# Re-queueing the mixers of a two-block kernel: sigmoids, gates, convolution taps and one-column sums

## The reference

```python
p_pool, p_bval, p_bgate, p_cgate, p_cx = jnp.split(_rmsnorm(h, mix_norm_g) @ w_in, splits, axis=-1)
# A: windowed means of p_pool, one small product, a scale
# B: u = p_bval * sigmoid(p_bgate); causal depthwise convolution of 31 taps over 256 channels;
#    layernorm over the channels; silu; one 256x256 product
# C: xc = 4-tap convolution of p_cx (512 channels); r, i = sigmoid(xc @ w_a + b_a), sigmoid(xc @ w_x + b_x)
#    log_a = -8 * r * softplus(-lam); a = exp(log_a); h = scan(a, sqrt(1 - a*a) * (i * xc)); gelu(p_cgate) * h
h = h + concat([A, B, C]) @ w_out
h = h + square(relu(_rmsnorm(h, mlp_norm_g) @ w_up)) @ w_down
```

## Time and profile before

| | before |
|---|---|
| median of 3 runs | 1047.05 us (1046.64 to 1047.58) |
| the profiled execution, its own time | 1047.22 us |
| its span, first to last instruction | 1045.3 us |
| busy PE, DVE, ACT, POOL | 98%, 49%, 40%, 55% |
| mean granted TensorE clock | 0.991 |

### The profile page before, as it was taken

One profiled execution on the slowest core, in us unless ns is written; L12 is line 12 of the kernel. 1 busy time (PEld: TensorE's weight loads), 2 busy tenths in 40 slices (PEclk: granted clock), 3 DMA queues, 4 the chain that ended last, 5 costly groups with the idle time before them and its releaser, 6 DMA issues.

```text
span 1045.3 us, 12713 instructions
## 1 busy us (share of the span) xinstructions
PE 1028.4 (98%) x5047; PEld 865.5 (83%) x5047; DVE 508.2 (49%) x835; ACT 421.0 (40%) x664; POOL 576.9 (55%) x724
## 2 busy tenths in 40 slices
PE   9999999999999999999999899999999999999997
PEld 7888888888888888888899877888888888888887
DVE  2781356665365633444778987457113213312323
ACT  5443445556534424443336573453213222212332
POOL 2655546555655774555535876365655554554551
PEclk9999999999999999999999899999999999999999
DMA  6323222122352215323223112322323232332312
GB/s 224 91 90 108 81 81 82 41 81 82 110 173 81 67 55 184 122 91 112 74 61 109 41 61 81 101 81 80 121 81 121 81 121 81 97 105 82 101 61 81
DMA packets 93500, 98.63 MB, mean 94 GB/s; under 512 B 3282, under 2 KB 88816, under 8 KB 93440
## 3 DMA queue, kind: packets, MB, share of 16 engines
q1 hardware_dynamic: 93440, 97.81, 29.0%
HBM read 95.71 MB, written 2.10 MB: 94 GB/s over the span
## 4 chain that ended last, share of the span: by engine, by line
PE 90%; DVE 5%; ACT 4%; issue 0%; DVEq 0%
PE ps L347 80%; PE ps L714 1%; DVE Fm L1079 1%; PE ps L695 1%; PE ps L1659 1%; PE ps L839 1%; DVE ps L1167 1%; PE ps L652 1%; PE ps L654 1%; PE ps L392 1%; ACT whi L263 1%; DVE Al L1567 1%; PE ps L445 0%; PE ps L1092 0%; ACT tmp L1176 0%; DVE Fm L1559 0%
## 5 line engine op out<-in xcount | busy, mean ns | idle before, releaser
L268 POOL TENSOR_TENSOR wlo<-raw,whi 128x256 fp32r<-128x256 f32 x668 | 507.9, 792 | 370.9 <-ACT whi L263 370.9
L347 PE MATMUL ps<-Hh,whi 128*128 128x512 f32 x832 | 329.4, 396 | 3.6 <-DVE Hl L1258 1.4
L347 PE MATMUL ps<-Hl,whi 128*128 128x512 f32 x832 | 325.2, 391 | 0.0
L263 ACT ACTIVATE whi<-raw 128x1024 fp32r<-128x1024 f32 x167 | 175.9, 1054 | 164.2 <-PE ps L347 151.0
L347 PE MATMUL ps<-Hh,wlo 128*128 128x512 f32 x832 | 209.6, 390 | 0.0
L347 PE MATMUL ps<-Ah,whi 128*128 128x512 f32 (+1 forms) x576 | 198.6, 368 | 0.2 <-DVE Al L1567 0.2
L347 PE MATMUL ps<-Al,whi 128*128 128x512 f32 (+1 forms) x576 | 196.0, 363 | 0.0
L347 PEld LDWEIGHTS ps<-Hh,whi 128*128 128x128 f32 x832 | 156.6, 188 | 39.7 <-DVE Hl L408 4.0
L347 PEld LDWEIGHTS ps<-Hh,wlo 128*128 128x128 f32 x832 | 156.8, 188 | 32.7
L347 PEld LDWEIGHTS ps<-Hl,whi 128*128 128x128 f32 x832 | 156.8, 188 | 31.7 <-issue 0.5
L347 PE MATMUL ps<-Ah,wlo 128*128 128x512 f32 (+1 forms) x576 | 125.6, 364 | 0.0
(11 more groups left out here) (295 smaller groups left out, 954.6 us busy)
## 6 DMA issues: line engine op xcount, KB each, us to landing
raw<-in_w_in SPq DMA_DIRECT2D x33, 1024.0 KB, 5.3
raw<-in_w_up SPq DMA_DIRECT2D x16, 1024.0 KB, 5.4
raw<-in_w_down SPq DMA_DIRECT2D x16, 1024.0 KB, 5.1
raw<-in_w_att_out SPq DMA_DIRECT2D x4, 1024.0 KB, 5.1
raw<-in_w_sg_out SPq DMA_DIRECT2D x4, 1024.0 KB, 5.3
raw<-in_w_o SPq DMA_DIRECT2D x4, 1024.0 KB, 5.1
raw<-in_w_in SPq DMA_DIRECT2D x6, 512.0 KB, 3.9
Fm<-in_x SPq DMA_DIRECT2D x2, 1024.0 KB, 6.9
```

The lines of the kernel that those rows point to most:

```text
L263: eh = A(lambda e, s=s, src=src, kk=kk: e.activation(wtile(whi, s, kk), src, ACT.Copy), raw_ev[b], used)
L268: el = G(lambda e, s=s, src=src, kk=kk, cut=cut: e.tensor_tensor(wtile(wlo, s, kk)[:, *cut], src[:, *cut], f(wtile(whi, s, kk))[:, *cut], ...
L347: return e.matmul(ps[:, bk, 0:c1 - c0], wt, x[:, k, c0:c1], start=st, stop=sp)
```

## The change

Six edits, all inside the second block's mixers.

1. A short list `soon` of pairs (count, function) is looked at in every step of `product`; a function is called when its count of steps has run out.
2. The eight one-column sums of the row factors are split: four at the middle of product 0, four with the whole chain of factors four steps later. Both spreads are emitted together two steps into product 1 (before: at its start and at its middle).
3. In branch C each tile's `rg_high`, `rg_low` stand behind the preceding gate, so ACT has the sigmoid ahead of the next high part. Tile 3's gates come half a product later.
4. All DVE taps of channel tile 0 are done early; those of tile 1 start after product 11 instead of product 7. Tile 1 has 20 DVE taps and 11 side taps. The second `pool_out` comes one product earlier, and `pool_high(1)` and `pool_low(1)` move ahead in their queues.
5. `conv_merge` adds the two channel tiles on DVE before the sums (two more DVE adds), so that 8 one-column matmul calls remain of 16, in two groups of four, four steps of W4 apart.
6. `conv_norm` comes ten steps after the second group.

```diff
+        def due():
+            while soon:
+                if soon[0][0]:
+                    soon[0][0] -= 1
+                    return
+                soon.pop(0)[1]()
...
                     if mid is not None and (g, n) == half_way:
                         mid()
+                    due()
...
             for col, acc, ev in sums:
+                if col:
+                    yield
...
-        N_DVE = 22
+        N_DVE = (22, 20)
...
         def conv_merge():
...
+            e1 = V(lambda e: e.tensor_tensor(tmp[:, i3, 0:512], cv[:, 0], cv[:, 1], ALU.add), ev[0], ev[1], f3)
+            e2 = V(lambda e: e.tensor_tensor(tmp[:, i1, 0:512], tmp[:, i1, 0:512], tmp[:, i2, 0:512], ALU.add),
+                   ea[0], ea[1])
...
+            next(last_sum)
+            soon.append([4, row_factors])
+            yield
+            soon.append([2, row_spreads])
+            yield
...
             cx(3, *made[7])
             side_tap(0)
-            taps(1, (1,))
+            taps(1, (0,))
             rg_conv(3)
+            yield
+            rg_gate(2, 0)
             rg_high(3)
-            taps(1, (1,))
+            taps(1, (0,))
             rg_low(3)
             rg_scan(1)
-            yield
-            rg_gate(2, 0)
             side_tap(1)
             yield
             rg_gate(2, 1)
             pool_in(0, *made[8])
             side_tap(0)
             rg_input(2)
             yield
-            rg_gate(3, 0)
             e3 = pool_mix(0)
             side_tap(1)
             yield
-            rg_gate(3, 1)
+            rg_gate(3, 0)
             pool_in(1, *made[9])
             ea = pool_high(0, e3)
+            es = pool_low(0, ea)
+            yield
+            rg_gate(3, 1)
             rg_exps(2)
             rg_input(3)
-            es = pool_low(0, ea)
-            yield
             e3 = pool_mix(1)
             side_tap(1)
+            ea = pool_high(1, e3)
             rg_root(2)
+            es1 = pool_low(1, ea)
...
+            conv_sum(*sums[0])
+
+            def second_sum():
+                got["cf"] = conv_factors(conv_sum(*sums[1]))
+
+            def norm():
+                got["cn"] = conv_norm(got["cf"])
+            soon.extend([[4, second_sum], [10, norm]])
```

More of the change, by code:

```diff
@@ L1327, in table, with row_factors @@
             A(lambda e: e.activation(sm[:, 107:108], ones[:, 0:1], fn), e_ones)
-        def mixers():
+        def row_factors():
             ended(last_sum)
@@ L1342, in mixers, with row_spreads @@
             e7 = A(lambda e: e.activation(rc, rc, ACT.Sqrt), e6)
-            sp2 = spread(Rb[:, 16:SM], rc[:, 4:8], 6, e7)
-            next(sp2)
+            got["sp"] = spread(Rb[:, 16:SM], rc[:, 4:8], 6, e7), spread(None, rc[:, 0:4], 7, e7)
+            for g in got["sp"]:
+                next(g)
             table(ACT.Sigmoid)
-            yield
[L1347 to L1351, removed]
+        def row_spreads():
+            e_r2 = ended(got["sp"][0])
+            got["R2"] = V(lambda e: e.tensor_copy(Rb[:, 0:16], sm[:, 42:58]), e_metaT, e_r2)
+            got["s0"] = sgt_scaled(0, *made[0])
+            got["R1"] = ended(got["sp"][1])
+        def mixers():
+            next(last_sum)
+            soon.append([4, row_factors])
+            yield
+            soon.append([2, row_spreads])
             yield
-            got["R1"] = ended(sp1)
-            sgt_times(0, s0)
+            sgt_times(0, got["s0"])
             rescale(0, 3)
@@ L1361, in mixers @@
             side_tap(0)
-            taps(4, (0,))
+            taps(3, (0,))
             yield
@@ L1381, in mixers @@
             rg_low(1)
-            yield
-            rg_gate(0, 1)
             side_tap(0)
-            taps(1, (0,))
+            rescale(5, 6)
             yield
@@ L1469, in mixers @@
             side_tap(1)
-            taps(1)
             cg_lo((1,))
             yield
-            e5 = pool_out(1, es1)
             scale_cg(2)
@@ L1477, in mixers @@
             cg_hi((2,))
-            pool_out_low(1, e5)
+            side_tap(1)
+            cg_lo((2,))
+            yield
+            side_tap(1)
             taps(1)
-            cg_lo((2,))
-            side_tap(1)
-            yield
-            taps(3)
-            side_tap(1)
             yield
@@ L1504, in mixers @@
             x1_add((2, 3), rec_mm)
-            taps(N_DVE)
-            merged = conv_merge()
+            taps(31)
+            sums = conv_merge()
             yield
             yield
-            sp = conv_sums(*merged)
-            yield
-            cn = conv_norm(sp)
+            conv_sum(*sums[0])
[4 more added lines that the diff above has]
+            soon.extend([[4, second_sum], [10, norm]])
             yield
             yield
-            conv_mix(cn)
+            yield
+            conv_mix(got["cn"])
         z0 = V(lambda e: e.memset(ub[:, :, 0:14], 0.0), e_f1)
```

54 lines of the change are left out of this document (28 added, 26 removed).

## The result

| | kernel before | kernel after |
|---|---|---|
| median of the runs | 1047.11 us (4 runs, 1046.64 to 1047.58) | 1039.48 us (4 runs, 1039.29 to 1039.95) |
| profiled execution: time, span | 1047.22, 1045.3 us | 1039.29, 1037.5 us |
| granted clock, mean | 0.991 | 0.997 |

The ratio is 0.9928 (95% interval 0.9911 to 0.9945): 7.6 us faster, where 9.2 were forecast. The page of the kernel after answers to the earlier trace rows: PE is as full as before, and DVE has a larger part in the chain (6%).

The account below looks back on a forecast made before the run. PE was busy 98% of the span, but DVE, nearly full up to the merges, limited what counts. 5.8 + 3.4 = 9.2 us off 1047.22 us gave 1038.0 us; the 8-of-10 range was 1034.0 to 1043.0 us.

Parts of the forecast that it names:

- DVE sets the sums: Up to the merges: DVE is nearly full, so PE's gain counts only as far as DVE follows.
- The rival in which PE sets the end: Whole stretch: DVE's pieces fit better, PE gains its own sum, about 14.4 us, giving 1032.8 us; chance 0.14.
- the slower one: Rival: the end moves to DVE's tail, last `cg_lo` at 635 or later, giving 1051.1 us; chance 0.05.
- Row factors, 1.65 us: Row factors' sums: two groups of eight rows avoid the half clock behind them, gaining 1.65 us.
- The first bound of that step: Row factors' sums: sixteen rows in a piece were followed by a fall of the clock.
- Gates, 1.5 us for tiles 0 and 1, nothing for tile 2: Gates: shorter waits gain 1.5 us at tiles 0 and 1; tile 2's 5.6 us for PE stay unseen at the end.
- Tile 3's conv 3.5 us early, merges 3.5 us early: DVE up to the merges: conv starts 3.5 us early; two taps fewer (1.6 us) offset by 1.6 us added idle time.
- the one on POOL against DVE: DVE beside POOL: two more POOL adds stretch DVE pieces by at most 1.8 us, counted only in the range.
- First sum 0.7 + 0.1 us behind the merges: Convolution's first sum: needs one more add, so sums begin about 645.1, 5.8 us early.
- The convolution's sums, 3.4 us: Convolution's sums: sixteen rows fewer save 1.75 us, no half clock behind them 1.65 us; spreads charged nothing.
- The clock falls all the same: Rival at both places of sums: grouping does not keep the clock up, 1.65 us each, 1041.3 us; chance 0.18.
- 5.8: Up to the convolution's first sum: gates, row factors and taps together make it 5.8 us early.

Follow-up runs that it names:

- e5: The changed kernel with two taps of tile 1 moved back from POOL to DVE (22 on DVE); median 1041.43 us.
- e6: The changed kernel with two further taps of tile 1 moved from DVE to POOL (18 on DVE); median 1039.13 us.
- e4: The changed kernel with only the order on ACT undone: high parts of tiles 1 and 3 again ahead of the sigmoids; median 1041.15 us.
- e10: The changed kernel with four POOL adds of side taps left out, so the output lacks these taps; median 1036.99 us.
- e1: The changed kernel with the second pool output and its low part one product later; median 1039.70 us.
- e2: The changed kernel with the row factors' sixteen one-column rows in one run again; median 1041.51 us.
- e11: The kernel before with only the row factors' part of the change (two groups of eight); median 1046.24 us, ratio 0.9995.
- e7: The kernel before with only the convolution's sums changed (two groups of eight rows, two adds ahead); median 1041.82 us.
- e9: The changed kernel with three side taps of tile 1 queued later, no work taken away; median 1038.54 us.
- e3: The changed kernel with the convolution's 32 rows in one run again and without the two adds; median 1042.39 us.
- e12: e9 with the second pool path ahead of the roots, two side adds after its low part, and normalization one product matmul later; median 1039.52 us.

## Why the prediction was right, and where its steps were off

*DVE sets the sums: right.* e5 and e6 show it at DVE's last pieces (two taps more there put the sums 1.14 us later, two fewer 0.55 earlier), e4 and e10 fit, and e1 doesn't tell. The rival in which PE sets the end is out, and so is the slower one: the last `cg_lo` ended just ahead of the nine taps of 629.30, not at 635 or later.

*Row factors, 1.65 us: right in size, open in frequency.* e2 puts the fall at 1.77 us, e11's profile at 1.79. But e7's profile shows that it doesn't come in each execution, and e11's median shows no gain that can be told from none. The first bound of that step ("sixteen rows in a piece were followed by a fall") is a statement on one execution.

*Gates, 1.5 us for tiles 0 and 1, nothing for tile 2: the sum is near, the split is wrong.* Undoing the order on ACT cost 1.64 us in all, though PE lost 3.9 us of waits and a low clock (e4). But at tiles 0 and 1 it is worth only 0.48 us, seen at tile 3's conv, and tile 2's order, which the forecast put at nothing because DVE would not come earlier by it, is worth about 1.2. That the two together come to what the forecast has for tiles 0 and 1 alone is luck. PE's wait of 1.47 us for tile 0's second sigmoid went mostly by other means: with the old order on ACT it is 0.2 us (e4). Tile 1's conv starts 1.3 us earlier than the row factors explain (25.92 us behind the first row-factor sum, from 29.01), and two taps and a rescaling piece that stood ahead of it on DVE now stand behind it. This move was not tested alone.

*Tile 3's conv 3.5 us early, merges 3.5 us early: the second part failed.* The conv came 4.61 us earlier (585.80 to 581.19), the merges only 3.18 (646.48 to 643.30). Of the 4.61, 0.36 are the earlier start of this execution, 1.77 the row factors (e2) and 0.48 the order on ACT (e4); the rest lies in the moves that no run undid alone. The step that failed is the one on POOL against DVE: it took nothing in the sum and at most 1.8 us in the range, from two adds more. The windows from tile 3's conv to the merges show it, of the kernel after and of the one before:

```profile
581.19:643.30 62.11, 55.58 (x272) 46.20 (x272) 58.16 (x65) 35.02 (x50) 54.36 (x52) 0.97 0.24 77
```

```profile
585.80:646.48 60.68, 54.66 (x263) 45.81 (x262) 55.29 (x67) 33.80 (x48) 48.17 (x48) 0.94 0.25 78
```

DVE does two taps fewer and yet is busy 2.87 us longer; with the taps' 1.6 us that is some 4.5 us of longer pieces. POOL is busy 54.36 us there, 6.19 more than before. The two added adds are not what did it: they stand beside the nine taps, which kept their length. What I overlooked is that moving DVE's work earlier moves it under POOL work that was there already. In the kernel before, the second pool mix ran while POOL had nothing to do (603.42 to 609.59, but for one add):

```profile
605.65 0.70 DVE L1233 TENSOR_TENSOR tmp<-Fm 128x527 f32<-128x527 f32 x1
606.39 1.44 DVE L1233 TENSOR_TENSOR tmp<-tmp 128x525 f32<-128x525 f32 x2
```

```profile
603.42 1.77 POOL L1181 TENSOR_TENSOR tmp<-tmp 128x512 f32<-128x512 f32 x1
609.59 3.59 POOL L268 TENSOR_TENSOR wlo<-raw,whi 128x256 fp32r<-128x256 f32 x4 [4.41 <-ACT whi L263]
```

In the change the same three pieces took 1.24 and 2.83 us. This is also what made PE's new wait as long as 5.6 us, since the low part it waits for stands behind them: with the adds later it is 2.6 us (e9), without them 1.7 (e10).

That the merges missed by only 0.3 us all the same is luck too. The forecast let DVE's idle time in this stretch grow by 1.6 us, from 5.39 (60.68 less 55.29) to 7.0; it fell to 3.95 (62.11 less 58.16). So 3.0 us less idle time and a conv 1.1 us earlier than forecast made up for most of the 4.5 us.

*First sum 0.7 + 0.1 us behind the merges: small, but set by another wait.* The add is done in time; PE's matmuls behind its wait for the second `x1_add` in W3 set the first sum (e3), at 645.72 and not 645.1.

*The convolution's sums, 3.4 us: oversized by 0.8.* In the kernel before, the same edit gives 3.22 (e7), near the term. In the change 0.58 of that is lost at the spreads, whose chain I charged nothing and priced at 0.3 if late: it was late, with DVE's two pieces at 2.23 us beside POOL's weight tile and at 1.26 behind it (e7).

*The clock falls all the same: didn't happen behind the groups* in the profile of the change, and its four runs lie within 0.7 us. e5 shows that it can, in an execution in which PE stood idle just ahead of them.

By these, 5.8 became 5.2 and 3.4 became 2.64. Undone one at a time, the row factors' grouping (1.77 us, in the profiled execution), the order on ACT (1.64) and the two taps (1.14) bring back 4.55 of the 4.84 us that lie between the row factors' and the convolution's sums; whether they add up so was not tested. The Trainium skill's rule that the fall goes with PE's standing idle ("TensorE: Matmul & The Clock Gate", section "HAM oscillation — how this bites in real kernels") fits the fall at 608, which begins inside PE's wait of 5.6 us, and may have a part in e5; no run here tests that part. It doesn't fit e3, where the clock is 0.67 from 650 to 655 with PE busy all the time behind 32 rows of sums, nor e2, where it is 0.63 from 528 to 532 in the same way.

## What to carry to other kernels

Before you credit a wait that a change removes, find the engine whose work must be done at the place where the time is set, and count only what reaches it; in e4 PE, busy for 98%, was 6.59 us later at tile 3's first gate, and the end saw 1.64. When a change moves a busy engine's work in time, look at what runs beside it at the new time: here pieces of 0.70 us became pieces of 1.24 to 1.79 beside POOL's work. When a forecast comes out, check its terms one by one: here errors in both directions nearly cancelled. And look at several executions before you treat a drop of the clock as part of the program.

## What the runs showed of the hardware

The roots on DVE, whose inputs both lie in on-chip memory outside the accumulator banks, had three durations: 0.70 us with POOL idle (e10), about 1.24 beside a weight tile on POOL, and 1.76 to 1.79 beside a side add (after, e12). Taps, which read the accumulator bank, stayed at 0.74 to 0.76 us each, POOL busy or not (before and after). A side add on POOL took 1.73 us beside such a root and 1.30 at 621.66 and 624.30 (after).

The clock behind sixteen one-column rows in a run fell in one profiled execution and not in another, with the same instructions (0.50 from 528.8 to 532.1 in the kernel before, 1.00 in e7).
